# A gated scan by levels: each level's score matmuls take the half of the query columns that is read, the last level also the half of the keys

## The chip, the cores and the metric

The kernel runs on one core of one Trainium2 chip, as one launch. The metric is the time of the device in microseconds, the median of several runs. The kernel computes two blocks of a model one after the other; the change touches one stage of the second block, the gated scan (`stage_hgrn_scan`), which runs four times: two layers, two directions.

## The reference

The scan is a chunked gated linear recurrence for 4 heads of 64 channels over 2048 positions (preceded, as a start of the state, by 256 context positions). Cut to what matters:

```python
def hgrn_scan(q, k, v, log_f, s0, with_output):       # S_t = diag(f_t) S_{t-1} + k_t v_t^T, o_t = S_t^T q_t
    def step(state, inp):
        qc, kc, vc, lf = inp
        a = jnp.cumsum(lf, axis=2)
        a_last = a[:, :, -1:, :]
        s_new = jnp.exp(a_last)[:, :, 0, :, None] * state + jnp.einsum(
            "bhsk,bhsv->bhkv", kc * jnp.exp(a_last - a), vc)
        inter = jnp.einsum("bhtk,bhkv->bhtv", qc * jnp.exp(a), state)
        diff = a[:, :, :, None, :] - a[:, :, None, :, :]
        dec = jnp.exp(jnp.where(causal, diff, -jnp.inf))
        scores = jnp.einsum("bhtk,bhsk,bhtsk->bhts", qc, kc, dec)
        intra = jnp.einsum("bhts,bhsv->bhtv", scores, vc)
        return s_new, inter + intra
```

It is done forward and backward (the second direction works on flipped sequences), in both layers; layer 0 also gives outputs for the context.

## The kernel before, in words

**Stages.** `program` issues the stages one after the other; a stage ends when all engines are done with it. The scan stage is called for layer 0 with the context's outputs (`out_ctx`, so `off` is 0) and for layer 1 without them (`off` is 1: the first step only builds the state).

**Steps, pairs, blocks.** A scan has five steps: one of n = 2 blocks of 128 positions (the context), then four of n = 4 blocks (512 positions). The four heads are two pairs `pr`; a pair's two heads lie in partitions 0 to 63 and 64 to 127, so head h uses one half of TensorE's rows. Pair 1 runs five phases behind pair 0 (`SKEW`), and each step of a pair has eleven phases (`PH`).

**Levels.** Within a block of 128 positions the masked score matrix (keys in the partitions, queries in the columns) is put together from eight products, phases 0 to 7, here L0 to L7. L0 is the diagonal. L1 pairs neighbours, and L2 to L7 pair halves of growing blocks: at level ph the block is made of pieces of x = 2^(ph-1) positions (x = 1 for L0 and L1), of which every other piece is a query piece (`qh`) and every other one a key piece (`kh`). Only the query pieces' columns (for L0 the `kh` ones) are read afterwards. `level` issues, at line 1732, one fp32 matmul per block and head: stationary operand the decayed keys `kb` (64 rows by 128 columns), moving operand the decayed queries (128 columns), output 128 by 128 into `ps_s`. Levels 0 and 1 read `qT` (shown in the trace as `features_or_outputs` or `y_t`), levels 2 to 7 read `qf`. In the trace one fp32 matmul is two LDWEIGHTS and two MATMUL records, so a level of n = 4 has 4 blocks x 2 heads x 2 = 16 records of each.

**Who keeps what.** For L0 to L5 VectorE copies the read columns under a mask into `scores_t` (`keep`, line 1902, two instructions a level). For L6 and L7 ScalarE copies rectangles (line 1816). After a level's matmuls VectorE also raises the decays: `raise_q` (line 1884) and `raise_k` (line 1891). Level ph + 1 waits for both: `up` (raised) and `cp` or `ca` (kept).

**The rest of a step on TensorE.** In phases 1 to 4 the next step's projection is spread, two k-slices each (line 1709, four records of 512 columns, on the whole array). Phase 8 turns the keys (line 1743), phase 9 forms the state's updates (line 1751), phase 10 the outputs (lines 1766 and 1775). The order on TensorE is that of `slots()`: one after the other the phase of pair 0 and that of pair 1. With the skew of five, half a step (all phases of slots 10 to 15, say) is one sequence for the older pair A and the younger pair B: L5 of A, L0 of B, L6 A, L1 B, projection B, L7 A, L2 B, projection, turn A, L3 B, projection, state A, L4 B, projection, outputs A, and then L5 of B. It is called a half-step here. In the last step of a scan there is nothing left to project.

Of the kernel before, what the change touches and what calls it, by code (L numbers as in the profile page):

```python
# [13 lines left out]
P = 128  # L14
# [1632 lines left out]
def stage_hgrn_scan(env, layer, d, hT, qT, vN, oT, out_ctx):  # L1647
# [8 lines left out]
    qh, kh = (0, 1) if d else (1, 0)  # L1656
    PH, SKEW, RS = 11, 5, 8
    HB = P // 2
# [5 lines left out]
    with ExitStack() as ctx:  # L1664
        f = env.sb(ctx, "f", [P, 2, 2, CH])
        kb = env.sb(ctx, "kb", [P, 2, 2, CH])
# [10 lines left out]
        pS = [env.banks(ctx, f"ps_s{i}", 2) for i in range(2)]  # L1677
# [7 lines left out]
        def slots():  # L1685
            for at in range(NSTEP * PH + SKEW):
                for pr in range(2):
                    x = at - SKEW * pr
                    if 0 <= x < NSTEP * PH:
                        yield (pr, *divmod(x, PH))  # L1690

        @block.sync
        def _(sp):
            env.load_groups(sp, g + 1 + 1)

        @block.tensor
        def _(pe):
            w = env.group_here(pe, g)

            def project(s, pr, ks):  # L1700
                col, n = steps[s]
                for k in ks:
                    if k == 0 and s >= 1:

                        pe.wait_ge(sg[pr].h, sg[pr].at(2 * s))
                    if k == 0 and s >= 2:

                        pe.wait_ge(su[pr].h, su[pr].at(blocks_to[s - 1]))
                    mm = pe.matmul(pf[pr][:, 0:n * P], w[:, k, pr * P:(pr + 1) * P], hT[:, k, col:col + n * P],
                                   start=(k == 0), stop=(k == KT - 1))  # L1710
                    if k == KT - 1:
                        mm.then_inc(pj[pr].h, 1)

            def level(s, pr, ph):
                col, n = steps[s]
                if s < off:
                    return
                if ph == 0:
                    pe.wait_ge(ready[pr].h, ready[pr].at(2 * s + 2))
                    if s > off:  # L1720
                        pe.wait_ge(ca[pr].h, ca[pr].at(2 * (s - off)))
                else:
                    pe.wait_ge(up[pr].h, up[pr].at(ups(s) + ph))
                    if ph <= 6:
                        pe.wait_ge(cp[pr].h, cp[pr].at(6 * (s - off) + ph))
                    else:
                        pe.wait_ge(ca[pr].h, ca[pr].at(2 * (s - off) + 1))
                for i in range(n):
                    for h in range(2):
                        lo = slice(HD * h, HD * (h + 1))  # L1730
                        q = qT[lo, pr, col + i * P:col + (i + 1) * P] if ph < 2 else qf[lo, pr, i * P:(i + 1) * P]
                        mm = pe.matmul(pS[pr][h][:, i * P:(i + 1) * P], kb[lo, s % 2, pr, i * P:(i + 1) * P], q,  # L1732
                                       start=True, stop=True)
                mm.then_inc(sc[pr].h, 1)

            def turn(s, pr):
                n = steps[s][1]
                pe.wait_ge(up[pr].h, up[pr].at(ups(s + 1)))
                if s + 1 < NSTEP:

                    pe.wait_ge(sg[pr].h, sg[pr].at(2 * s + 4))
                for i in range(n):
                    mm = pe.transpose(pf[pr][:, i * P:(i + 1) * P], kb[:, s % 2, pr, i * P:(i + 1) * P], env.ident[:, :])
                mm.then_inc(tm[pr].h, 1)

            def state(s, pr):
                col, n = steps[s]
                pe.wait_ge(tc[pr].h, tc[pr].at(s + 1))
                for i in range(n):
                    for h in range(2):  # L1750
                        mm = pe.matmul(pf[pr][HD * h:HD * (h + 1), i * HD:(i + 1) * HD],
                                       kbn[:, pr, i * P + HD * h:i * P + HD * (h + 1)],
                                       vN[:, col // P + i, pr * P + HD * h:pr * P + HD * (h + 1)], start=True, stop=True)
                mm.then_inc(um[pr].h, 1)

            def outputs(s, pr):
                col, n = steps[s]
                if s < off:
                    return
                pe.wait_ge(cp[pr].h, cp[pr].at(6 * (s - off) + 6))  # L1760
                pe.wait_ge(ca[pr].h, ca[pr].at(2 * (s - off) + 2))
                if s > off:
                    pe.wait_ge(oc[pr].h, oc[pr].at(s - off))
                for i in range(n):
                    for h in range(2):
                        pe.matmul(pO[pr][HD * h:HD * (h + 1), i * P:(i + 1) * P],
                                  vN[:, col // P + i, pr * P + h * HD:pr * P + (h + 1) * HD],
                                  sT[:, pr, h, i * P:(i + 1) * P], start=(i == 0), stop=False, skip_group_check=True)
                for x, i in enumerate(range(n - 1, -1, -1) if d else range(n)):
                    nd = blocks_to[s] + x  # L1770
                    if nd >= 1:
                        pe.wait_ge(su[pr].h, su[pr].at(nd))
                    for h in range(2):
                        lo = slice(HD * h, HD * (h + 1))
                        mm = pe.matmul(pO[pr][lo, i * P:(i + 1) * P], st[lo, pr, nd % RS, :], qf[lo, pr, i * P:(i + 1) * P],
                                       start=False, stop=True, skip_group_check=True)
                mm.then_inc(om[pr].h, 1)

            pe.wait_ge(env.sem("state_zero").h, env.sem("state_zero").at(1))
            for pr in range(2):  # L1780
                project(0, pr, range(KT))
            for pr, s, ph in slots():
                if ph < 8:
                    level(s, pr, ph)
                elif ph == 8:
                    turn(s, pr)
                elif ph == 9:
                    state(s, pr)
                else:
                    outputs(s, pr)  # L1790
                if s + 1 < NSTEP and 1 <= ph <= 4:
                    project(s + 1, pr, (2 * ph - 2, 2 * ph - 1))
            for pr in range(2):
                pe.wait_ge(om[pr].h, om[pr].at(NSTEP - off))
            pe.sem_inc(env.sem("w_used").h, 1)
# [1538 lines left out]
```

## Time and profile before

| What | us |
|---|---|
| median of 3 runs | 5157.46 |
| lowest and highest of them | 5143.28, 5161.43 |
| the profiled execution's own time | 5149.12 |
| its span | 5147.2 |
| TensorE matmuls busy | 4681.0 (91%) |
| VectorE busy | 2559.2 (50%) |
| ScalarE busy | 1803.3 (35%) |
| line 1732, matmuls on kept queries (L2 to L7), busy | 235.0 |

How to read it: the span is that of the program on the device, the execution's own time lies 1.9 us above it.
### The profile page before, as it was taken

How to read it: one execution, taken by the hardware profiler on the slowest of the kernel's cores; microseconds unless marked ns; L12 is line 12 of the kernel's file. 1: busy time of each engine (PE TensorE's matmuls, PEld its weight loads, DVE VectorE, ACT ScalarE, POOL GpSimd, SP SyncE). 2: the span in 40 equal slices, each digit the busy share in tenths (PEclk: the TensorE clock that was granted, in tenths of full speed). 3: DMA queues.
4: the chain of work that ended last, by engine and by line, in shares of the span. 5: the costliest groups of instructions: out<-in, count | busy, mean ns of one | idle time of the engine just before them, and what ended most of it. 6: DMA issues, size and time to landing. Idle time of an engine off the chain costs nothing. (4 is left out here: it accounts for less than half of the span.)

```text
span 5147.2 us, 68637 instructions
## 1 busy us (share of the span) xinstructions
PE 4681.0 (91%) x26733; PEld 3333.5 (65%) x26733; DVE 2559.2 (50%) x5125; ACT 1803.3 (35%) x3422; POOL 1237.6 (24%) x1247
## 2 busy tenths in 40 slices
PE   6998998997969989899998998999888999989989
PEld 3447777786758656754556776877656745556767
DVE  3332345666744556444554365444655545533654
ACT  3332224554344111223434443243112224444431
POOL 1000021102410101417883000001222448850000
PEclk8999999998979999999999999999998999999999
DMA  5012103334430000100000212210000100002122
GB/s 196 8 41 82 49 1 128 122 123 168 170 111 17 9 10 1 53 21 11 11 9 16 82 35 86 89 39 17 2 9 20 48 9 11 11 13 70 44 81 91
DMA packets 149685, 272.02 MB, mean 53 GB/s; under 512 B 11628, under 2 KB 82676, under 8 KB 147700
## 3 DMA queue, kind: packets, MB, share of 16 engines
q1 hardware_dynamic: 145044, 257.14, 14.9%
q10 hardware_dynamic: 4320, 10.49, 0.6%
q8 instruction: 215, 3.52, 0.3%
q14 instruction: 106, 0.87, 0.1%
HBM read 198.40 MB, written 69.19 MB: 52 GB/s over the span
## 5 line engine op out<-in xcount | busy, mean ns | idle before, releaser
L1515 PE MATMUL ps_proj<-features_high,weights_high 128*128 128x512 f32 (+1 forms) x1168 | 471.1, 403 | 53.3 <-DVE features_low L1581 50.6
L1515 PE MATMUL ps_proj<-features_high,weight_ring_low 128*128 128x512 f32 (+1 forms) x1168 | 450.4, 386 | 0.0
L1515 PE MATMUL ps_proj<-features_low,weights_high 128*128 128x512 f32 (+1 forms) x1168 | 443.4, 380 | 0.0
L1581 DVE TENSOR_TENSOR features_low<-h_t,features_high 128x512 fp32r<-128x512 f32 (+2 forms) x300 | 224.3, 758 | 251.2 <-ACT features_high L1545 250.5
L1581 DVE TENSOR_TENSOR features_low<-features_or_outputs,features_high 128x512 fp32r<-128x512 f32 (+1 forms) x248 | 200.1, 816 | 229.6 <-ACT features_high L1545 229.2
L1515 PEld LDWEIGHTS ps_proj<-features_high,weights_high 128*128 128x128 f32 x1168 | 222.4, 190 | 120.6 <-issue 38.8
L1732 PE MATMUL ps_s<-qf,kb 64*128 64x128 f32 x3264 | 235.0, 284 | 60.9 <-DVE scores_t L1902 55.5
L1545 ACT ACTIVATE features_high<-h_t 128x512 fp32r<-128x512 f32 (+2 forms) x300 | 198.7, 665 | 256.0 <-PE ps_proj L1515 229.4
L2513 ACT ACTIVATE weight_ring<-ps_st 128x1024 f32<-128x1024 f32 x193 | 197.7, 1024 | 249.2 <-PE ps_st L2400 243.6
L1732 PEld LDWEIGHTS ps_s<-qf,kb 64*128 64x128 f32 x3264 | 200.3, 188 | 112.2 <-issue 59.5
L1545 ACT ACTIVATE features_high<-features_or_outputs 128x512 fp32r<-128x512 f32 (+1 forms) x248 | 176.3, 714 | 229.5 <-PE ps_proj L1515 204.2
L1515 PEld LDWEIGHTS ps_proj<-features_low,weights_high 128*128 128x128 f32 x1168 | 225.5, 193 | 45.9
L1515 PEld LDWEIGHTS ps_proj<-features_high,weight_ring_low 128*128 128x128 f32 x1168 | 222.6, 191 | 46.0 <-issue 7.6
L3007 PE MATMUL ps_o<-w_out_high,y_high 128*128 128x512 f32 x544 | 217.0, 399 | 28.7 <-DVE y_low L3025 21.1
L2561 DVE TENSOR_REDUCE features_or_outputs<-ps_max 128x2 f32<-128x1024 f32 x128 | 156.7, 1224 | 166.3 <-PE ps_max L2370 166.3
L2561 DVE TENSOR_REDUCE y_t<-ps_max 128x2 f32<-128x1024 f32 x128 | 156.7, 1224 | 156.8 <-PE ps_max L2370 156.8
L728 PE MATMUL ps_proj<-weights_high,features_high 128*128 128x512 f32 x512 | 206.8, 404 | 27.8 <-DVE features_low L823 27.8
L2543 POOL TENSOR_TENSOR features_or_outputs<-features_or_outputs,weight_ring 128x512 f32<-128x512 f32 x176 | 223.3, 1289 | 33.6 <-ACT weight_ring L2513 31.1
L2543 POOL TENSOR_TENSOR y_t<-y_t,weight_ring 128x512 f32<-128x512 f32 x176 | 223.2, 1289 | 33.5 <-ACT weight_ring L2513 31.1
L1129 ACT ACTIVATE scores<-scores,row_stats 128x256 f32<-128x256 f32 (+1 forms) x384 | 172.5, 450 | 144.6 <-DVE row_stats L1076 144.6
L3007 PE MATMUL ps_o<-w_out_low,y_high 128*128 128x512 f32 x544 | 213.6, 393 | 0.0
L3007 PE MATMUL ps_o<-w_out_high,y_low 128*128 128x512 f32 x544 | 213.5, 392 | 0.0
(436 smaller groups left out, 10370.8 us busy)
## 6 DMA issues: line engine op xcount, KB each, us to landing
weight_ring<-in_w_in_dram SPq DMA_DIRECT2D x40, 1024.0 KB, 5.6
weight_ring<-in_w_mod_dram SPq DMA_DIRECT2D x48, 512.0 KB, 4.1
x_res<-h_rows SPq DMA_DIRECT2D x32, 512.0 KB, 3.5
res<-result SPq DMA_DIRECT2D x48, 264.0 KB, 2.1
res_rows<-res SPq DMA_DIRECT2D x48, 264.0 KB, 3.9
h_t<-v_rows SPq DMA_DIRECT2D x3, 4096.0 KB, 13.9
q_rows<-q_rows SPq DMA_DIRECT2D x34, 256.0 KB, 2.6
x_rows<-in_x_dram SPq DMA_DIRECT2D x16, 512.0 KB, 9.9
```

Of the source, the lines that this page charges most:

```text
L728: mm = pe.matmul(out[:, :], f_[:, k, i * P:(i + 1) * P], w_[:, k0 + k, :], start=(k0 + k == 0 and n == 0), stop=(k0 + k == KT - 1 and n == 2))
L1129: act.activation(pr[:, u % 2, 2 * b + j, 0:w * P], sc[:, u % 2, 2 * b + j, 0:w * P], ACT.Exp, bias=stat[:, (u // 2) % 4, h:h + 1], scale=-1.0,
L1515: mm = pe.matmul(bank[:, 0:n], w_[:, k0 + k, i * P:(i + 1) * P], f_[:, k, 0:n], start=start, stop=stop)
L1545: act.activation(self.fh[:, s % NB, :, 0:n], self.hT[:, k0:k0 + KS, c0:c0 + n], ACT.Copy).then_inc(self.fhs.h, 1)
L1581: dve.tensor_tensor(self.fl[:, s % NB, :, 0:n], self.hT[:, k0:k0 + KS, c0:c0 + n], self.fh[:, s % NB, :, 0:n].bitcast(F32), ALU.subtract). ...
L1732: mm = pe.matmul(pS[pr][h][:, i * P:(i + 1) * P], kb[lo, s % 2, pr, i * P:(i + 1) * P], q, start=True, stop=True)
L2513: act.activation(pT[s % 3], sT[s % 2][:, :, :], ACT.Exp, scale=HD ** -0.5).then_inc(ex.h, 1)
L2543: pool.tensor_tensor(acc[g % 2][:, kv, :], before, pT[s % 3][:, kv, :], ALU.add).then_inc(pa.h, 1)
L2561: ins = dve.tensor_reduce(part[:, g % 2, t, c, :].rearrange("p (v i) -> p v i", v=2)[:, :, i], pM[:, :, 0:n], AXX, ALU.max)
L3007: mm = pe.matmul(ps[i % 2][half][:, :], y[:, i % 2, k, :], w[:, k, sl], start=(k == 0 and n == 0), stop=(k == KT - 1 and n == 2))
```

## The change

`used` takes, out of every group of 2x columns, the x columns that are read: for the moving operand and for the output. The matmul so has 64 moving columns instead of 128, in runs of x columns with gaps of x (at L7 one run of 64). At L7, where x is 64, the keys are cut too: `rows` are the 64 key columns of the half `kh`, so the stationary operand has 64 columns and the output 64 partitions. At L0 to L6 the stationary operand stays whole. Nothing else differs: not the number of matmuls, nor their order, nor what is waited for.

```diff
@@ level(), TensorE
+                x = 1 << max(ph - 1, 0)
+                rows = slice(HB * kh, HB * (kh + 1)) if x == HB else slice(0, P)
+                used = lambda t: t.rearrange("p (b a x) -> p b a x", a=2, x=x)[:, :, kh if ph == 0 else qh, :]
                 for i in range(n):
                     for h in range(2):
                         lo = slice(HD * h, HD * (h + 1))
                         q = qT[lo, pr, col + i * P:col + (i + 1) * P] if ph < 2 else qf[lo, pr, i * P:(i + 1) * P]
-                        mm = pe.matmul(pS[pr][h][:, i * P:(i + 1) * P], kb[lo, s % 2, pr, i * P:(i + 1) * P], q,
+                        mm = pe.matmul(used(pS[pr][h][rows, i * P:(i + 1) * P]),
+                                       kb[lo, s % 2, pr, i * P + rows.start:i * P + rows.stop], used(q),
                                        start=True, stop=True)
```

On TensorE, in the first half-step in which both pairs work on four blocks, the instructions stand as follows (a row is a line's matmuls of one shape, output partitions by columns; `ps_s_130` and `ps_s_131` are pair 0's and pair 1's score banks, and a shape such as 2x32 means two runs of 32 columns; one row entry is one fp32 matmul, two records in the trace):

```order
-L1732 MATMUL ps_s_130<-qf,kb 128x128 x8
-L1732 MATMUL ps_s_131<-qf,kb 128x128 x8
+L1735 MATMUL ps_s_130<-qf,kb 64x64 x8
+L1735 MATMUL ps_s_131<-qf,kb 128x32x2 x8
 L1709 MATMUL ps_f_129<-h_t,weight_ring 128x512 x2
-L1743 MATMUL ps_f_129<-ident,kb 128x128 x4
-L1732 MATMUL ps_s_131<-qf,kb 128x128 x8
+L1747 MATMUL ps_f_129<-ident,kb 128x128 x4
+L1735 MATMUL ps_s_131<-qf,kb 128x16x4 x8
```

The two rows at the top are L7 of the older pair and L2 of the younger one; L7 now has 64 partitions by 64 columns, L2 keeps its 128 partitions and has 32 runs of 2 columns. No instruction has moved; lines after the edit are four higher, and the score matmul stands at line 1735.

## Rows read from the trace of the kernel before

**Rows 1.** The page, busy time by engine: the kernel's span

```profile
span 5147.2 us, 68637 instructions
```

**Rows 2.** Windows, two scans: length, PE, PEld, DVE, ACT, POOL busy, PE clock, DMA, GB/s

```profile
1674.20:1881.40 207.20, 181.80 (x1780) 126.56 (x1780) 119.06 (x308) 36.61 (x100) 21.83 (x70) 0.97 0.02 6
...
3746.00:3937.00 191.00, 168.46 (x1618) 116.58 (x1616) 113.98 (x274) 29.61 (x79) 43.70 (x90) 0.96 0.01 2
```

**Rows 3.** Timeline of TensorE, one half-step: start us, length, instructions [idle before]

```profile
1749.66 1.16 PE L1732 MATMUL ps_s<-qf,kb 64*128 64x128 f32 x16
...
1752.45 1.16 PE L1732 MATMUL ps_s<-qf,kb 64*128 64x128 f32 x16 [0.73 <-DVE scores_t L1902]
1753.98 1.16 PE L1732 MATMUL ps_s<-features_or_outputs,kb 64*128 64x128 f32 x16 [0.38 <-DVE scores_t L1902]
1755.08 1.98 PE L1709 MATMUL ps_f<-h_t,weight_ring 128*128 128x512 f32 x4
1756.99 2.06 PE L1732 MATMUL ps_s<-qf,kb 64*128 64x128 f32 x32
1758.98 1.98 PE L1709 MATMUL ps_f<-h_t,weight_ring 128*128 128x512 f32 x4
...
1764.33 0.69 PE L1751 MATMUL ps_f<-features_or_outputs,kb_rows 128*64 128x64 f32 x16
1764.95 1.16 PE L1732 MATMUL ps_s<-qf,kb 64*128 64x128 f32 x16
...
1770.00 1.16 PE L1732 MATMUL ps_s<-qf,kb 64*128 64x128 f32 x16
```

**Rows 4.** Timeline of TensorE, last step of a scan: L7 of A, L2 of B

```profile
1836.40 1.16 PE L1732 MATMUL ps_s<-qf,kb 64*128 64x128 f32 x16
1838.29 1.16 PE L1732 MATMUL ps_s<-qf,kb 64*128 64x128 f32 x16 [0.72 <-DVE scores_t L1902]
```

**Rows 5.** Windows: the last step, the end of the scan, and dilated attention

```profile
1836.40:1852.06 15.66, 11.12 (x166) 9.56 (x165) 11.78 (x29) 2.17 (x6) 2.28 (x7) 1.00 0.00 1
1865.00:1872.00 7.00, 3.24 (x43) 2.73 (x40) 2.95 (x8) 1.71 (x6) 0.00 (x0) 0.96 0.00 0
1872.00:1880.00 8.00, 5.34 (x51) 4.20 (x49) 1.69 (x5) 1.19 (x2) 0.00 (x0) 0.61 0.02 2
1140.00:1200.00 60.00, 60.00 (x463) 47.18 (x461) 38.27 (x219) 36.87 (x175) 0.00 (x0) 1.00 0.54 178
```

**Rows 6.** Lines by source: durations ns min/median/max of weight loads and matmuls

```profile
L1732 PEld LDWEIGHTS ps_s<-qf,kb x3264: 182/188/335, 1688.8 to 3927.7; 64*128 64x128 f32 x192
L1732 PE MATMUL ps_s<-qf,kb x3264: 271/272/579, 1688.8 to 3927.9; 64*128 64x128 f32 x192
...
L1751 PEld LDWEIGHTS ps_f<-features_or_outputs,kb_rows x288: 132/138/227, 1707.4 to 2079.2; 128*64 128x64 f32 x144
L1751 PE MATMUL ps_f<-features_or_outputs,kb_rows x288: 222/222/368, 1707.4 to 2079.2; 128*64 128x64 f32 x144
...
L992 PEld LDWEIGHTS ps_score<-k_t,q_t x256: 287/308/311, 1100.8 to 1200.8; 64*128 64x128 f32 x128
```

**Rows 7.** Timeline of TensorE in the first block's dilated attention, dilation 16

```profile
1153.15 1.14 PE L992 MATMUL ps_score<-k_t,q_t 64*128 64x128 f32 x8
1154.22 0.65 PE L1036 MATMUL ps_pv<-weight_ring 128*64 128x256 f32 x4
1154.80 1.10 PE L1023 MATMUL ps_pv<-h_t,cos 128*128 128x64 f32 x8
1155.74 0.61 PE L1006 MATMUL ps_pt<-ident,scores 128*128 128x128 f32 x4
```

**Rows 8.** Timeline of VectorE, same half-step: kept scores of L2 and L3

```profile
1759.77 1.29 DVE L1902 COPY_PREDICATED scores_t<-level_masks,ps_s 128x256 f32<-128x256 uint8 x2
...
1763.21 0.76 DVE L1902 COPY_PREDICATED scores_t<-level_masks,ps_s 128x256 f32<-128x256 uint8 x2
```

**Rows 9.** Timeline of TensorE, end of the fourth scan: a level at the lower clock

```profile
3926.24 2.06 PE L1732 MATMUL ps_s<-qf,kb 64*128 64x128 f32 x16 [1.29 <-ACT scores_t L1816]
```

## The prediction

> **What bounds the kernel now.** I started with the page: the span is 5147.2 us [rows 1], and TensorE is its busiest engine. The windows over the scans come next. A scan of layer 0 takes 207.2 us and one of layer 1 takes 191.0, and matmul records are open in 181.8 and 168.5 us of them, against 119.1 and 114.0 us of VectorE [rows 2]. Inside a half-step the timeline of TensorE gives the order and the stops: from L5 of one pair (1749.66) to L5 of the other (1770.00) are 20.34 us, in which TensorE waits twice only, 0.73 us before L6 and 0.38 us before L1, both times for VectorE's kept scores [rows 3]. So here time goes as TensorE's work goes, but for 1.1 us. In a scan's last step, which has no projections, it is different: L2 waits 0.72 us for VectorE, where in the steady half-step it waited for nothing [rows 4], and matmul records are open 11.1 of 15.7 us, as long as VectorE is busy, 11.8 us [rows 5]. There a chain binds that runs level, VectorE, next level.
>
> How much of it is this line? The kept-query levels L2 to L7 have 3264 records [rows 6], that is 544 for each level, and 544 / 16 = 34 levels of four blocks (the context's half-size ones counted as halves). So there are 34 half-steps' worth of eight levels: 26 with projections, 8 (two a scan) without.
>
> **What a level costs, and of what.** Two levels in a row take 1.99 us (1756.99 to 1758.98), one takes 1.10 us (1753.98 to 1755.08) [rows 3]. The second one thus costs 0.89 us. That is 8 pairs of records, one record of either head, of 112 ns each, and 0.2 us go to the passage from half rows to the whole array. The question is what these 112 ns are: 128 columns streamed, which the change halves, or a weight load, which it leaves alone in L0 to L6.
>
> - A load of 128 columns has a record of 188 ns, one of 64 columns 138 ns [rows 6]: 50 ns for 64 columns (56 by the shortest, 188 against 132), so 100 to 112 ns for 128. Head 0's and head 1's loads run beside each other: in the dilated attention the load reads every sixteenth element and its record is 308 ns [rows 6], 120 longer, hence some 230 ns. Its eight records take 1.07 us (1153.15 to 1154.22) [rows 7]; less 0.2 that is 218 ns a pair, one load and not two. That shape is this line's but for the stride, and where the load got longer the pair got longer with it. So a load is not hidden beyond its own length, and 112 ns is what a plain one takes.
> - The row nearest to the new shape is line 1023: 128 weight columns and 64 moving columns. Eight of its records take 0.94 us (1154.80 to 1155.74) [rows 7], 117 ns each, 112 without a small handover. With half the columns the step is still one load.
>
> So for L0 to L6 I take the pair at 112 ns, unchanged. The two ends are 117 ns (line 1023 as it stands) and 58 ns (a pair of line 1751, with 64 weight columns and 64 moving ones: 16 records in 0.62 us, 1764.33 to 1764.95 [rows 3], some 0.15 of it handover).
>
> [...]
>
> **The sum, term by term.**
>
> 1. L7 gets 64 weight and 64 moving columns, the shape of line 1751: 1.10 us become 0.62, or 0.43 by the pairs (8 x 54 ns); I take 0.45. On the path in a steady half-step: L2 of B stands behind it in the queue, then a projection, the turn and L3. L3 needs VectorE's kept L2 (done at 1759.77 + 1.29 = 1761.06 [rows 8]), but that copy itself follows L2 and moves with it. Not on the path in the last step: L2 waits there for kept L1, 0.72 us after TensorE is free [rows 4], and an earlier L7 only lengthens that wait. Of eight full L7 in a scan two lie so (one from each of the two last-step half-steps), the very last one is alone and on the path. So 6 x 4 scans x 0.45 = 10.8 us, and the context's four half-size ones 4 x 0.22 = 0.9: **11.7 us**.
> 2. The last matmul of every level ends sooner: 272 ns for 128 columns, 222 for 64 [rows 6], so 0.05 us where VectorE or ScalarE is waited for. In a steady half-step that is once (the run of VectorE work from L5 to L1, which holds both stops of [rows 3]): about 24 x 0.05 = 1.2. In the last step it is five levels (L5, L1, L2, L3, L4) in 8 half-steps, 40 x 0.05 = 2.0, and in the heads and tails of the four scans four levels each, 0.8. **4.0 us**.
> 3. The passage to the projection behind L1 to L4, 112 times, could lose the same 0.05 us each, if the whole array waits for the stream's end: 0 to 5.6 us. The trace doesn't show it apart; I take **1 us**, since line 1023's step leaves a short stream no effect.
> 4. VectorE, ScalarE, POOL and the queues do what they did: the same elements of the same banks are read, no DMA is touched, nothing new is waited for. Nothing, and it is not cover but the same work.
>
> Together 16.7 us. With a pair at 117 ns in L0 to L6 it is 7 levels x 8 x 5 ns x 26, or 7 us less; with the full 5.6 us of term 3 it is 5 us more: 9 to 22 us. The profiled execution took 5149.1 us, so the same one would take 5132; it lies 8.3 us below the median of the runs shown, and against that median, 5157.5, the change gives **5140 us**, 0.33% less. A measurement of this kernel can tell about 0.5%, 26 us, from no change, so this is "same".
>
> **The rivals.**
>
> *Levels halve after all* (the load hides beside work of the other head). Each level loses 8 x 54 ns = 0.43 us. Steady half-steps: 3.4 us less work, but VectorE's chain from L5 to L1 (two raises, two copies, one raise, two long copies) stays and the two stops grow; L3 then sits at the kept L2. Following the queue through, 20.34 becomes about 17.8 us: 26 x 2.6 = 68. Last steps: five levels on the chain, 8 x 5 x 0.43 = 17. Tails 3. That is 88 us: **5070 us**. For it: plain pairs at 112 ns fit a stream of 128 columns as well. Against it: [rows 7]. Halfway (a pair near 85 ns) it is 5113.
>
> *Strides cost.* L0 and L1 read and write every second column, L2 two of four. Kept scores show such a thing on VectorE, in the same banks: two copies take 1.29 us at runs of 2, 0.76 us at runs of 4 [rows 8], a factor 1.7; the strided load gives 230 / 110 = 2.1. On a stream of 64 columns, 56 ns, that is 95 to 118 ns: hidden by the load, or 6 ns a pair above it, 5 us in all, **5145 us**. At a factor of 2.5 it eats the gain, at 4 it adds 3 levels x 34 x 0.9 us = 92, 5232. The Trainium skill (Advanced Engine Details and Errata, PSUM Cachelines) says that access patterns in PSUM that aren't contiguous slow matmuls significantly, pairs of fp32 being the unit; it gives no figure, and no row of before has a matmul with such an output.
>
> *The clock drops in the last step* (slower than before). With half the columns TensorE does less. In the last step records are already open only 71% of the time at a granted clock of 1.00, 2.4 GHz; in the tail, at 46%, it is 0.96, and 0.61 right after [rows 5], on its way to 1.2 GHz. A level then takes 2.06 us instead of 1.16 [rows 9]. If the last step of each scan fell to 1.2 GHz, each half-step would pay five levels x 0.9 and some 1.7 for the outputs, 6.2 us; 8 of them 50, the tails 6 more: 56 against 17 gained, +39, **5196 us**. It decides once the granted clock of the last step leaves 1.00 for more than a third of it. Against it: in dilated attention the records of line 1023 with 64 columns stand among loads just as long and the clock stays 1.00 [rows 5].
>
> **How the numbers follow.** Forecast 62% (5 of them, by spread of the runs, beyond 0.5% faster, 1 slower); levels halve 12%, halfway 9% (8 faster by over 0.5%, 1 within); strides 9% (5 within, 4 slower); clock 8%. Faster by over 0.5%: 5 + 12 + 8 = 25%. Slower: 1 + 4 + 8 = 13%. Within: 62%. The forecast's own range is 5122 to 5157 (9 to 22 us, and the spread of runs from 5143 to 5161). The range reaches down to 5100 for the halfway case and up to 5180 for light strides and a part of the clock's case; it leaves out full halving (12), the heavy strides (4) and half of the clock's case (4).
>
> **What would show it.** Right: in the steady half-step two levels L7 and L2 in a row take about 1.55 us instead of 1.99, single levels still 1.05 to 1.10, the half-step about 19.8; load records 188 ns at L0 to L6 and about 135 at L7; matmul records 222. Wrong: single levels at 0.65 us (first rival), L0 and L1 longer than L3 (strides), a granted clock under 1.00 in the last step (clock). I am wrong in the main if a pair of L3 to L6 takes under 100 ns.

## The result: slower, by the clock, and half of it in a place that no rival had named

The changed kernel takes 5237.6 us (median of 5 runs, 5233.9 to 5249.8) against 5157.5 (5 runs, 5143.3 to 5163.6): 1.0148 times as long, 95% interval 1.0129 to 1.0167. The forecast was 5140 us, its range ended at 5180.

The page of the profiled execution (5234.5 us): the span, TensorE's busy row and the row of the granted clock in 40 slices, in tenths.

```profile
span 5232.7 us, 68637 instructions
...
PE 4776.8 (91%) x26733; PEld 3404.2 (65%) x26733; DVE 2557.6 (49%) x5125; ACT 1804.1 (34%) x3422; POOL 1237.9 (24%) x1247
...
PEclk8999999998979878799999999999887999999999
```

VectorE, ScalarE and POOL are busy as long as before; TensorE's matmul records are open 96 us longer, with the same number of instructions and half the columns in this line. The clock's row has two dips at the scans. The windows over the four scans (length, then PE, PEld, DVE, ACT, POOL busy, granted clock) show how much of it lies there:

```profile
1676.28:1903.17 226.89, 203.56 (x1781) 142.29 (x1781) 118.69 (x308) 36.64 (x100) 21.81 (x70) 0.82 0.02 6
1903.17:2133.51 230.34, 209.43 (x1781) 146.45 (x1781) 123.26 (x316) 32.66 (x92) 21.81 (x70) 0.79 0.01 4
3603.17:3814.67 211.50, 188.98 (x1621) 132.53 (x1621) 109.99 (x268) 33.51 (x86) 44.99 (x90) 0.81 0.02 6
3814.67:4024.55 209.88, 189.06 (x1620) 132.32 (x1621) 113.52 (x274) 30.05 (x80) 43.80 (x90) 0.81 0.01 4
```

Measured between the same two starts (first projection to the next stage's first matmul) the four took 207.2, 201.6, 192.5 and 192.5 us before, 793.8 together, and take 878.6 now. That is 84.8 of the 85.5 us by which the span grew. The first one stands beside [rows 2]: 226.9 for 207.2 us, at a granted clock of 0.82 for 0.97.

Inside a half-step, TensorE's timeline (start us, length, instruction, idle before it), which answers to [rows 3]:

```profile
1754.56 1.11 PE L1735 MATMUL ps_s<-qf,kb 64*128 64x64 f32 x16
1755.50 1.06 PE L1735 MATMUL ps_s<-features_or_outputs,kb 64*128 64x64 f32 x16
1757.29 1.11 PE L1735 MATMUL ps_s<-qf,kb 64*128 64x64 f32 x16 [0.73 <-DVE scores_t L1906]
1758.82 1.80 PE L1735 MATMUL ps_s<-features_or_outputs,kb 64*128 64x64 f32 x16 [0.43 <-DVE scores_t L1906]
1760.55 3.78 PE L1709 MATMUL ps_f<-h_t,weight_ring 128*128 128x512 f32 x4
1764.26 2.41 PE L1735 MATMUL ps_s<-qf,kb 64*64 64x64 f32 x32
1766.60 1.98 PE L1709 MATMUL ps_f<-h_t,weight_ring 128*128 128x512 f32 x4
...
1768.95 1.11 PE L1735 MATMUL ps_s<-qf,kb 64*128 64x64 f32 x16
1769.99 1.98 PE L1709 MATMUL ps_f<-h_t,weight_ring 128*128 128x512 f32 x4
```

L5, L0, L6 and L1 stand here one after the other, with the two stops. In L1 the matmuls turn slow, the projection behind it takes 3.78 us instead of the 1.98 of [rows 3], and L7 with L2 2.41; then everything is at its old pace, until the next such stretch. Cut out as windows, with the last step as the fourth:

```profile
1754.56:1760.55 5.99, 4.84 (x67) 4.50 (x65) 4.14 (x10) 2.65 (x7) 0.00 (x0) 0.87 0.01 3
1760.55:1766.60 6.05, 6.05 (x38) 3.33 (x37) 2.39 (x5) 0.65 (x2) 0.00 (x0) 0.56 0.00 0
1766.60:1777.52 10.92, 10.92 (x99) 6.72 (x97) 6.29 (x16) 0.60 (x1) 2.28 (x7) 1.00 0.01 2
...
1847.71:1864.86 17.15, 14.72 (x132) 12.90 (x133) 9.26 (x24) 1.94 (x6) 2.29 (x7) 0.50 0.00 1
```

A granted clock of 0.50 is the lower of TensorE's two levels, 1.2 GHz. Before, it was 1.00 through the whole last step [rows 5] and through the whole half-step:

```profile
1749.66:1770.00 20.34, 19.23 (x199) 13.13 (x197) 12.82 (x31) 3.89 (x10) 2.27 (x7) 1.00 0.01 2
```

The half-steps now take 22.96 us (1754.56 to 1777.52) and 21.48 (1777.52 to 1799.00) in turn, against 20.34; in the last step L2 to L4 and the outputs take 1.97 us each at the lower level:

```profile
1859.15 1.97 PE L1735 MATMUL ps_s<-qf,kb 64*128 64x64 f32 x16 [0.56 <-DVE scores_t L1906]
1861.06 1.97 PE L1770 MATMUL ps_o<-scores_t,features_or_outputs 128*64 128x128 f32 x16
```

Added up from the traces, half-step by half-step over the four scans: each scan has five steady half-steps, in which both pairs work on four blocks and projections stand between the levels. These 20 take 38 us longer, 1.9 each. The eight last-step half-steps take 37 us longer: from L7 of A (1849.58) in one of them to that of the other (1871.03) are 21.5 us, against 16.75 before (1836.40 to 1853.15). The starts of the scans take 7 us longer, most of it in the first half-steps behind the context (17.77 before, 20.43 and 20.63 now), and the tails 2. That makes 85, the growth of the four scans. The forecast's 26 half-steps with projections are counted by work and include the partly filled ones at the starts; 20 of them stand in the trace in the full form.

### The profile page after: what moved, and what is told of

Read it like the earlier page. It is cut to its first block and busy times, and to the rows that moved or that the text cites. A ratio compares the mean times of both kernels' runs of the same rounds, so it can differ in the third digit from the quotient of the medians.

```text
span 5232.7 us, 68637 instructions
## 1 busy us (share of the span) xinstructions
PE 4776.8 (91%) x26733; PEld 3404.2 (65%) x26733; DVE 2557.6 (49%) x5125; ACT 1804.1 (34%) x3422; POOL 1237.9 (24%) x1247
## 5 line engine op out<-in xcount | busy, mean ns | idle before, releaser
L1735 PEld LDWEIGHTS ps_s<-qf,kb 64*128 64x128 f32 (+1 forms) x3264 | 222.7, 210 | 121.4 <-issue 72.2
L1735 PE MATMUL ps_s<-qf,kb 64*128 64x64 f32 (+1 forms) x3264 | 251.7, 303 | 52.7 <-DVE scores_t L1906 47.3
```

The costliest lines, as they stand in the source:

```text
L1735: mm = pe.matmul(used(pS[pr][h][rows, i * P:(i + 1) * P]), kb[lo, s % 2, pr, i * P + rows.start:i * P + rows.stop], used(q), start=True, s ...
```

## The experiments

Theory A: with half the columns TensorE streams too little between L5 and the projection, the clock falls to 1.2 GHz there, and the loss is what the matmuls behind it take at that level. The rivals: the narrow tile of L7; the strides; any halved level, wherever it stands; the stops by themselves. All times of before in a comparison are from the same chip and hours (5160 to 5165 us).

**L7 alone.**

```diff
+                cut = ph == 7
-                used = lambda t: t.rearrange(...)[:, :, kh if ph == 0 else qh, :]
+                used = lambda t: t.rearrange(...)[:, :, kh if ph == 0 else qh, :] if cut else t
```

> Only L7 is cut (64 keys by 64 query columns); L0 to L6 have 128 columns as before. Theory A (the clock falls because L0 to L6 stream half the columns around VectorE's two stops): the clock stays 1.00 in the half-steps and the kernel gains what L7 alone is worth, 24 full levels of 0.35 to 0.45 us and the small ones, so 9 to 13 us less than before, ratio 0.9975 to 0.9985. Rival B (the smaller stationary tile of L7 is what unsettles the clock or the queue): the projection behind L1 takes 3.7 us here too and the kernel is 50 us or more slower.

Measured: 5147.5 us, ratio 0.9973 (0.9960 to 0.9986), some 14 us less than before. The clock is 1.00 in the half-steps, and the projection behind L1 takes 1.98 us:

```profile
1808.48 1.16 PE L1736 MATMUL ps_s<-features_or_outputs,kb 64*128 64x128 f32 x16 [0.38 <-DVE scores_t L1907]
1809.58 1.98 PE L1709 MATMUL ps_f<-h_t,weight_ring 128*128 128x512 f32 x4
1811.49 1.77 PE L1736 MATMUL ps_s<-qf,kb 64*64 64x64 f32 x32
1813.19 1.98 PE L1709 MATMUL ps_f<-h_t,weight_ring 128*128 128x512 f32 x4
```

So rival B falls, and the one part of the change that was to gain does gain (the ratio is a little better than the expected 0.9975 to 0.9985). L7 and L2 take 1.70 us (1811.49 to 1813.19) for 1.99: 0.29 us, less than the 0.45 of the forecast.

**The cut between the projections, and the cut around the stops.** Two kernels that share the eight levels between them.

```diff
+                cut = ph in (2, 3, 4, 7)      # the first kernel
+                cut = ph in (0, 1, 5, 6)      # the second, with all keys in L7
```

> L2, L3, L4 and L7 are cut, L0, L1, L5 and L6 have 128 columns as before: the cut levels stand between projections, the uncut ones around VectorE's two stops. Theory A, in the form that the place decides: the clock stays 1.00 in the half-steps with projections; 0.35 to 0.45 us a half-step from L7 and 0.05 behind each of L2, L3 and L4; about 12 to 18 us less than before in all if the last steps hold their clock too, 0 to 15 us more if they do not, since there are no projections there. Rival C (any half columns lower the clock, wherever they stand): a projection near 3.7 us in every half-step and 40 us or more slower.

> L0, L1, L5 and L6 are cut to 64 columns, L2, L3, L4 and L7 are as before. Theory A by place: the clock falls as in the changed kernel, the projection behind L1 takes 3.7 us, and without L7's gain the kernel is as slow as the changed one or slower, 5225 to 5260 us. Rival C (the sum over the half-step decides): half of the effect, 5175 to 5205 us. Rival D (the columns do not matter, L7 does): 5150 to 5160 us.

Measured: the first 5166.1 us, ratio 1.0010 (0.9997 to 1.0022); the second 5226.3 us, ratio 1.0121 (1.0101 to 1.0140). In the first the clock is 1.00 in the half-steps with projections and L3 and L4 lose 0.05 us each; in the last step it falls behind L2, and the gain is lost there: its two half-steps take 19.46 and 19.83 us in the first scan instead of 16.75 and 16.50, and over the four scans that is 24 us, more than the 15 expected at most. The second has the changed kernel's picture, and nearly its whole loss. From it L1 and the projection:

```profile
1807.63 1.66 PE L1736 MATMUL ps_s<-features_or_outputs,kb 64*128 64x64 f32 x16 [0.42 <-DVE scores_t L1907]
1809.22 3.78 PE L1709 MATMUL ps_f<-h_t,weight_ring 128*128 128x512 f32 x4
```

The place decides: four halved levels cost nothing where projections stand between them, four others around the two stops 61 us (rival C, a half effect for half the levels, and D fall).

**One run of columns instead of pieces.**

```diff
+                cut = s > off + 1 or ph == 7
+                used = lambda t: t[:, 0:HB] if cut and x != HB else (t[:, HB * qh:HB * (qh + 1)] if cut else t)
```

> The cut of the changed kernel, but in L0 to L6 the 64 columns that are multiplied and written are the first 64 of each block in one run instead of every other piece; the first two steps that give scores keep all columns in L0 to L6. So half of the scores of the later steps is left out. Theory A: in the last three steps of layer 0 and the last two of layer 1 the levels take 1.04 us and the projection behind L1 3.7 us, as with strides. Rival E (strided reading or writing costs or lowers the clock): the clock stays at 1.00 there and single levels change from 1.04 us.

Measured, one run: 5209.2 us. In the steps with the cut, L3 is at 1.04 us (1809.83 to 1810.87) and the projection behind L1 slow, as with pieces:

```profile
1809.83 1.11 PE L1736 MATMUL ps_s<-qf,kb 64*128 64x64 f32 x16
1810.87 1.98 PE L1709 MATMUL ps_f<-h_t,weight_ring 128*128 128x512 f32 x4
...
1822.66 1.97 PE L1736 MATMUL ps_s<-features_or_outputs,kb 64*128 64x64 f32 x16 [0.42 <-DVE scores_t L1907]
1824.56 3.78 PE L1709 MATMUL ps_f<-h_t,weight_ring 128*128 128x512 f32 x4
```

All eight half-steps in which both pairs have such levels fall, as with pieces. Strides have no part in it (rival E falls). The Trainium skill's rule on PSUM (Advanced Engine Details and Errata, PSUM Cachelines), that an access pattern with gaps slows matmuls, isn't seen here: in the changed kernel L3 with runs of 4 takes the same 1.04 us (1768.95 to 1769.99) as this one run of 64. A cost hidden under the weight load would not show, so this says nothing on a matmul whose stream is its bound.

**Only half of the keys, with all or half of the columns.**

```diff
+                cut = False                   # the first kernel; in the second: s > off + 1
+                rows = slice(HB * kh, HB * (kh + 1)) if s > off + 1 else slice(0, P)
```

> From the third step that gives scores on (the third of layer 0's five, the third of layer 1's four), every level multiplies only the kh half of the key columns, 64 weight columns, but all 128 query columns; half of the scores of these steps is left out. Theory A1 (moving columns hold the clock): clock 1.00, a level still 1.05 to 1.10 us, the half-step near 20.3 us; bounded by the stream of 128 columns now. Rival A2 (the clock counts the cells or weights at work): the projection behind L1 takes up to 3.7 us here too.

> In the same steps every level has 64 weight columns and 64 moving columns, the read pieces; half of the keys' scores is left out. Load theory: at full clock a level takes 0.62 us and two in a row about 1.1, against 1.04 with 128 weight columns, so it is the load that kept L0 to L6 from gaining. Rival (something else, the instructions' issue, bounds a level of 16 records): near 1.0 us. The clock falls at least as far as in the changed kernel in either case.

Measured, one run each: 5140.5 and 5135.1 us. Two levels in a row, and the half-step, of the first (64 weight columns, 128 moving) and of the second (64 and 64), and the second one's levels around the stops:

```profile
1792.61 1.96 PE L1736 MATMUL ps_s<-qf,kb 64*64 64x128 f32 x32
1794.51 1.98 PE L1709 MATMUL ps_f<-h_t,weight_ring 128*128 128x512 f32 x4
```

```profile
1787.52 1.15 PE L1736 MATMUL ps_s<-qf,kb 64*64 64x64 f32 x32
1788.60 1.98 PE L1709 MATMUL ps_f<-h_t,weight_ring 128*128 128x512 f32 x4
...
1800.91 0.68 PE L1736 MATMUL ps_s<-qf,kb 64*64 64x64 f32 x16 [1.16 <-DVE scores_t L1907]
1802.44 0.68 PE L1736 MATMUL ps_s<-features_or_outputs,kb 64*64 64x64 f32 x16 [0.84 <-DVE scores_t L1907]
1803.05 1.98 PE L1709 MATMUL ps_f<-h_t,weight_ring 128*128 128x512 f32 x4
```

Two levels take 1.90 us with 64 weight columns and 128 moving, 1.08 with 64 and 64, and a single one 0.61 (1802.44 to 1803.05). With 128 weight columns and 64 moving a single one takes 1.04 (the changed kernel). So a level shrinks to about half only where both sides are halved: with 64 moving columns the load is what bounds L0 to L6, as the forecast had it, and the instructions' issue is not.

The first kernel keeps its clock: the projection behind L1 takes 1.98 us in every half-step with halved keys, and the half-step 19.81 us at 1.00 (1785.27 to 1805.08), half a microsecond less than expected. Halved weights alone do not lower the clock (rival A2 falls).

The second one keeps it in part. In the first scan its half-steps take 17.45 us at 1.00. But of the eight half-steps with projections in which both pairs have halved levels, three, in the second and third scan, take some 19.1 us at 0.91. In the second scan, L1 and the projection, and the window of the half-step:

```profile
1964.25 1.02 PE L1736 MATMUL ps_s<-features_or_outputs,kb 64*64 64x64 f32 x16 [0.85 <-DVE scores_t L1907]
1965.20 3.27 PE L1709 MATMUL ps_f<-h_t,weight_ring 128*128 128x512 f32 x4
...
1960.13:1979.12 18.99, 16.83 (x199) 10.35 (x195) 13.34 (x32) 3.41 (x9) 2.09 (x7) 0.91 0.01 2
```

The expectation, a fall at least as far as in the changed kernel, still misses: there every steady half-step falls. With 64 moving columns the pace matters: the same columns are spread over 5.3 us with whole loads (1777.52 to 1782.82 in the changed kernel) and over 4.6 with halved ones (1798.44 to 1803.05), though the stops are longer here (1.16 and 0.84 us).

**A longer stop, all columns.** VectorE keeps L5 twice.

```diff
+                if ph == 5:
+                    ins.then_inc(again[pr].h, 1)
+                    dve.wait_ge(again[pr].h, again[pr].at(s - off + 1))
+                    for h in range(2):
...
+                        ins = dve.copy_predicated(dst, mask, src)
```

> All levels whole as before, but VectorE keeps L5 twice, so that TensorE's stop before L6 is 0.7 to 0.8 us longer. If the share of time in which columns stream between L5 and L1 decides, whatever lowers it: the longer stop brings it from about 63% to 55%, a small step, and the clock may stay 1.00, the half-step 21.0 to 21.1 us and the kernel 18 to 25 us slower. If stops by themselves unsettle the clock: a projection of 3.7 us here too and 60 us or more slower.

Measured, one run: 5190.4 us, 29 more than before. The stop is 1.52 us. One half-step takes 21.13 us at 1.00. The one before it takes 22.76 us (1769.49 to 1792.25), with its projection at 3.20 us; its window below leaves out the first 1.5 us:

```profile
1771.00:1792.25 21.25, 19.36 (x175) 12.43 (x173) 13.28 (x33) 2.49 (x8) 2.27 (x7) 0.92 0.01 2
1792.25:1813.38 21.13, 19.23 (x199) 13.12 (x197) 13.59 (x33) 3.89 (x10) 2.27 (x7) 1.00 0.00 1
```

The stop itself costs 0.79 us a half-step (21.13 for 20.34), some 22 us in the 20 steady and 8 last-step half-steps, and the fall, in 5 of the 20 steady half-steps, 1.63 us each (22.76 for 21.13), some 8. So a longer stop with whole columns makes the clock fall too, though only in some half-steps.

**Columns put back, stops taken away, half of the cut.** Three kernels against the changed one.

```diff
+            def fill(s, pr, ph):                                # the first kernel
+                col, n = steps[s]
+                if s > off:
+                    pe.wait_ge(oc[pr].h, oc[pr].at(s - off))
+                pe.matmul(pO[pr][:, 0:n * HB], w[:, 0, 0:P], hT[:, 0, col:col + n * HB], start=True, stop=True)
...
+                if ph in (1, 6) and s >= off:
+                    fill(s, pr, ph)
...
+                m = 1 if ph in (0, 5) and s > off else n        # the second, in keep(); m blocks are kept
...
+                cut = ph in (0, 5)                              # the third, with all keys in L7
```

> The changed kernel, with all its cuts, and one more fp32 matmul in front of each L6 and each L1: 256 columns of the projection's operands on the whole array, written to the free output bank and never read. It streams 0.43 us of columns in each of the two stops, some 0.55 us with its load. Theory A (the share of time in which columns stream between L5 and the projection decides the clock): the share rises from about 32% to 45-48%, most projections behind L1 are back at 1.98 us, and although TensorE does more the kernel is faster than the changed one by 30 to 60 us: 5175 to 5205. Rival (the halved levels themselves, not the time without columns, lower the clock): no projection comes back and the added work makes it 5240 us or more.

> The changed kernel, but from the second step that gives scores on VectorE keeps only the first block of L0 and L5, so the stops before L6 and L1 nearly vanish; three quarters of these two levels' scores are left out. Theory A: the same 64 columns a matmul, a shorter stretch of low streaming, so the clock is 1.00 in most half-steps with projections and these take 18.5 to 19.2 us instead of 21.5 to 23. Rival (half columns at whole loads suffice, with no stop at all): the projection behind L1 still takes 3.7 us.

> Only L0 and L5, the two levels in front of the first stop, have 64 columns; L6, L1 and all others are whole. The streamed share between L5 and the projection lies halfway, near 47%. Theory A: the clock falls in some half-steps and not in others, 10 to 40 us slower than before. Rival (a threshold in what one level streams, any cut level lowers the clock): as the kernel that cuts all four, 60 us slower; or no fall at all, within 5 us of before.

Measured: 5175.2 us, ratio to before 1.0026 (1.0011 to 1.0040); 5158.6 us and 5157.5 us (one run each). The first is the clearest. It is the changed kernel with more work for TensorE, and it is 62 us faster:

```profile
1786.85 1.11 PE L1735 MATMUL ps_s<-qf,kb 64*128 64x64 f32 x16
1787.79 1.06 PE L1735 MATMUL ps_s<-features_or_outputs,kb 64*128 64x64 f32 x16
1788.78 0.70 PE L1744 MATMUL ps_o<-h_t,weight_ring 128*128 128x256 f32 x2
1789.59 1.11 PE L1735 MATMUL ps_s<-qf,kb 64*128 64x64 f32 x16
1790.62 0.70 PE L1744 MATMUL ps_o<-h_t,weight_ring 128*128 128x256 f32 x2
1791.25 1.11 PE L1735 MATMUL ps_s<-features_or_outputs,kb 64*128 64x64 f32 x16
1792.29 1.98 PE L1709 MATMUL ps_f<-h_t,weight_ring 128*128 128x512 f32 x4
```

The added matmul of line 1744 stands where the stops were, and the projection is back at 1.98 us. The half-step takes 19.92 us at a clock of 1.00. What is left of the loss lies in the last step, where the two added matmuls don't suffice (its window from L7 on, 1832.14 to 1849.00, has 0.60). The second kernel has the changed one's matmuls and short stops: a half-step of 18.75 us at 1.00, so the stops are needed for the fall too. It holds its own comparison: in the first two steady half-steps of each layer 1 scan a stop is still 0.7 us long, and there the projection is slow (3.68 us at 3604.25), while in the 16 others it is at 1.98. In its last step the clock falls as well (22.21 us for one half-step against 16.50 before), so its 5158.6 us mix gain and loss. The third, with two of the four levels halved, does not fall in the steady half-steps, 20.28 us at 1.00; I had expected some falls.

The last column counts the steady half-steps in which the clock falls, seen by a projection behind L1 of more than 1.98 us.

| Kernel | moving, weight columns of L5, L0, L6, L1 | L5 to projection, us | steady half-steps that fall |
|---|---|---|---|
| before | 128, 128 | 5.42 | 0 of 20 |
| changed | 64, 128 | 5.99, 5.30 at full clock | 20 of 20 |
| cut around the stops | 64, 128 | 5.85 | 19 of 20 |
| L0 and L5 cut | two with 64, 128 | 5.36 | 0 of 20 |
| both sides halved | 64, 64 | 4.61 | 3 of 8 |
| short stops | 64, 128 | 4.27 | 0 of 16 |
| stops filled | 64, 128 and 2 x 256 | 5.44 | 0 of 20 |
| longer stop | 128, 128 | 6.20 | 5 of 20 |

**A version that keeps what gains.** L7 cut, L2 to L4 cut where a projection follows.

```diff
+                cut = ph == 7 or (ph in (2, 3, 4) and s + 1 < NSTEP)
```

> L7 always cut, L2, L3 and L4 cut only where a projection stands behind them, L0, L1, L5, L6 and the whole last step (but L7) with 128 columns. Theory A (the clock falls where few moving columns stream between stops): granted clock 1.00 in all half-steps; 0.05 us behind each of L2 to L4 on top of L7's gain, so 14 + 3 to 4 = 17 to 18 us less than before, ratio 0.9965. Rival: the cut of L2 to L4 costs something even at full clock: no better than L7 alone, 0.9973 or worse.

Measured: 5148.4 us, ratio 0.9971 (0.9959 to 0.9983). The half-step takes 19.90 us at 1.00, 0.44 less than before; against L7 alone (20.05) that is the 0.15 of three shorter passages, but the two kernels' ratios can't be told apart.

**Columns where there were none.** The same, but with whole columns in the two L7 of each scan that are off the path, and in the tail of each scan a matmul in each stop whose result is never read.

```diff
+                cut = (ph == 7 and (s, pr) not in ((NSTEP - 2, 1), (NSTEP - 1, 0))) or (ph in (2, 3, 4) and s + 1 < NSTEP)
...
+            def fill(s, pr, c):
+                col, n = steps[s]
+                pe.wait_ge(oc[pr].h, oc[pr].at(s - off))
+                pe.matmul(pO[pr][:, 0:c], w[:, 0, 0:P], hT[:, 0, col:col + c], start=True, stop=True)
...
+                if s == NSTEP - 1 and pr == 1 and 6 <= ph <= 9:
+                    fill(s, pr, 4 * P if ph < 8 else 2 * P)
```

> L7 cut where it is on the path, L2 to L4 cut where a projection stands behind them, and in the tail of each scan, where one pair is alone, one more fp32 matmul in each of four stops (512 columns ahead of L6 and L7, 256 ahead of the turn and of the state), never read. Theory A: the streamed columns hold 2.4 GHz through the tail, so the turn takes 0.66, the state 0.69 and the outputs 1.09 us each instead of 1.12, 1.12 and 1.92: 3 us a scan, and 1 to 2 us more where the next stage starts warm; 10 to 18 us beyond the version without the extra matmuls, ratio 0.994 to 0.9955. Rival (the extra matmuls cost what they hold, or the clock falls all the same): 0.997 or worse.

Measured: 5132.4 us, ratio 0.9938 (0.9924 to 0.9951), 30 us less than before; its interval ends below that of the version without the added matmuls, and the ratio is a little better than the expected 0.994. From the last L5 to the next scan's first projection, first before, then in this kernel:

```profile
1864.25:1881.48 17.23, 9.33 (x102) 7.71 (x101) 5.98 (x14) 3.50 (x9) 0.00 (x0) 0.80 0.08 22
```

```profile
1862.62:1876.77 14.15, 9.42 (x111) 6.33 (x109) 5.98 (x14) 3.50 (x9) 0.00 (x0) 0.97 0.10 29
```

The granted clock is 0.97 for 0.80. Over the four scans the same stretch takes 17.23, 12.89, 17.13 and 16.40 us before and 14.15, 12.41, 14.15 and 12.42 here, 10.5 us less together. The second is the exception: in that trace of before its clock was 1.00 to begin with (2070.18 to 2083.07). Against the version without the added matmuls the four scans are 7.3 us shorter in the traces, of the 16 us between the medians; where the rest lies is not shown.

## Why the prediction was wrong, point by point

1. *What bounds the scans*: right. The stops, their sizes and the two kinds of half-step came out as read: 0.73 us ahead of L6 and 0.43 ahead of L1 (0.38 before).
2. *The load bounds L0 to L6*: right, and the terms that follow from it. Single levels take 1.04 us, the record of a load is 188 ns, and none of these levels halved. The first rival (5070 us) is out; the kernel with both sides halved shows that it would have needed the keys cut too. One reading on the way was wrong: "56 by the shortest" sets a median, 188 ns, against a shortest record, 132; the two shortest are 182 and 132 [rows 6], so both ways give 50 ns for 64 columns and 100 for 128. The pair at 112 did not hang on it.
3. *Term 1, L7*: the sign is right, the size too large. Two levels in a row went from 1.99 to 1.70 (L7 alone) or 1.65 us, not to about 1.55: the passage from L7's narrow tile to L2's wide one costs what one between equal tiles doesn't. Two equal narrow ones take 1.08.
4. *Terms 2 and 3, the shorter last stream*: 0.05 us are there behind every level that a projection follows (1.04 for 1.09, and the half-step of 19.90 us). Term 3 was thus undervalued at 1 us of 5.6. The size of the sum is borne out where the clock holds, though not closely: two kernels with parts of the change measure 14 and 15 us less, by their intervals 7 to 21 and 9 to 21, and their four scans are 9.3 and 13.1 us shorter in the traces.
5. *"The clock drops in the last step"*: the mechanism is the right one, at 8%, and two things in it failed. Its place was drawn too narrow. It was priced for 8 half-steps, 50 us, and in these it took 37; 38 more came from the 20 steady ones, and 9 from the starts and tails, of which the steady ones and the starts never stood under it. And the reason against it was a false likeness. I set the 64-column records of the dilated attention beside the new levels because both were load-bound, but in that stretch TensorE never stops, 60.00 of 60.00 us open [rows 5], and other matmuls stand between those records. The stretch to compare was the kernel's own, L5 to the projection, with two stops.
6. *The step that failed* is so in the sum: its terms run the half-steps with projections at the full clock, with the pairs of L0 to L6 "at 112 ns, unchanged" and nothing for TensorE's clock, and no reason is given for that nothing. The runs put in its place 1.9 us more in each of 20 steady half-steps, at granted clocks of 0.85 and 0.92: 38 us where the sum had a gain. The share of time with an open record, by which the rival weighed the last step, would not have shown it: in the steady half-step it is 19.23 of 20.34 us before and 21.81 of 22.96 after. It can't tell a pair that is bound by its load from one that streams all the time: a pair of 64 and 64 columns takes some 59 ns ((1.08 - 0.61) / 8 in the kernel with both sides halved), so by this estimate the stream has about half of the 112 ns of a pair with 64 moving columns.

The Trainium skill (TensorE: Matmul & The Clock Gate, the table "Why this matters for your kernels") names idle gaps between bursts as what lowers the clock. The trace goes further: the longest stop of the steady half-step is the same 0.73 us before and after, and only the columns in the levels around it changed. Where the page's table and the runs differ, the runs decide.

What is shown is that halved moving columns at the pace of a whole load, together with the stops, bring the clock down: taking away either (whole columns around the stops, or short stops) or filling the stops brings it back. That the amount of streaming is what counts is argued from the order of the kernels in the table. What stays open is the law behind it: the longer stop with 128 columns fell in 5 of 20 half-steps, both sides halved with 64 columns in 3 of 8. That the granted clock alternates between two patterns of half-step (22.96 and 21.48) was not tried either.

## What to carry to other kernels

Ask of a matmul first whether its stream or its weight load is the longer; if it is the load, cutting moving columns bought nothing here but 0.05 us at a level's end. And such a cut can cost: columns that nobody reads may be what holds TensorE at 2.4 GHz across the stops of another engine. So cut where dense work stands around, leave whole what lies beside waits, and read the granted clock in windows of a few microseconds before and after every saving on TensorE.

## What the runs showed of the hardware that was not expected

A kernel became 62 us faster by two added fp32 matmuls in each half-step, whose outputs are never read (5237.6 to 5175.2 us), and another some 16 us faster with four such matmuls in each scan's tail and two L7 near the end of each scan left whole (5148.4 and 5132.4 us, ratios to before 0.9971 and 0.9938; the two differences were not tried apart). The fall comes late: in the half-steps shown L5, L0 and L6 are still at full pace, and what pays is the dense projection behind them, 3.78 us for 1.98. Moving operands and outputs in pieces of 1, 4 and 8 fp32 columns or in one run of 64 made no difference to a level's 1.04 us.
